# A gated hybrid decoder layer on one core: where the high and low halves of Q, K and the value differences are made, and how far ahead the weight forms stand

## The reference

```
h = rms_norm(x);  u_pool, z_pool, q, k, v, z_attn, gate_logits = split(h @ w_in)
y_pool = pool_mixer(u_pool) * silu(z_pool)            # means over 2, 4, 8, 16 tokens
attn   = stick_breaking(q, k, v)                      # 8 heads of 64, keys before the query only
y_attn = attn * silu(z_attn);  gates = sigmoid(gate_logits + b)
x = x + (gates[0] * (y_pool @ w_pool_up) + gates[1] * (y_attn @ w_attn_up)) @ w_out
return rms_norm(x, final_g)
```

## Time and profile before

| | |
|---|---|
| median of three runs | 1765.09 us |
| the profiled execution | 1765.54 us, of it the span 1763.6 us |
| mean granted TensorE clock | 0.971 |
| stage 2 | 119 to 396 us |
| stage 3 | 396 to 1391 us |
| busy: TensorE, weight loads, VectorE, ScalarE, GpSimd | 1629.8, 1340.2, 1135.2, 787.7, 1016.7 us |

### The profile page before, as it was taken

How to read it: one execution, slowest core, us unless ns; L and a number is a source line. 1 busy time by engine, 2 the same in 40 slices (tenths; PEclk the granted TensorE clock), 3 DMA queues, 4 the chain that set the end, 5 groups by cost and what they waited for, 6 DMA issues and landing times. The chain is left out here.

```text
span 1763.6 us, 25448 instructions
## 1 busy us (share of the span) xinstructions
PE 1629.8 (92%) x8030; PEld 1340.2 (76%) x8030; DVE 1135.2 (64%) x1506; ACT 787.7 (45%) x1544; POOL 1016.7 (58%) x777
## 2 busy tenths in 40 slices
PE   7999999995988988989978899898899989999998
PEld 6878888883877867768767778777778778888886
DVE  6736428903876877868878777778877774242323
ACT  4412223322565655556655566655566542111111
POOL 3521116625677888787876887888877441414140
PEclk8999999998998999999989999999999999999999
DMA  6743226765232223232474323332222575434331
GB/s 233 230 153 132 73 96 238 268 212 185 71 92 72 85 79 101 78 92 81 136 265 165 99 85 97 93 87 82 87 70 69 178 226 178 134 128 137 135 97 72
DMA packets 142679, 228.85 MB, mean 130 GB/s; under 512 B 46929, under 2 KB 63825, under 8 KB 142562
## 3 DMA queue, kind: packets, MB, share of 16 engines
q1 hardware_dynamic: 142562, 227.42, 39.8%
HBM read 149.76 MB, written 77.60 MB: 129 GB/s over the span
## 5 line engine op out<-in xcount | busy, mean ns | idle before, releaser
L1547 DVE TENSOR_TENSOR_SCAN left<-keep,left 128x512 f32<-128x512 f32 x192 | 305.0, 1589 | 72.8 <-issue 51.7
L1362 PE MATMUL psum<-hT,ring 128*128 128x512 f32 x644 | 268.8, 417 | 31.7 <-POOL ring L1612 27.3
L1366 PE MATMUL psum<-hT,ring 128*128 128x512 f32 x644 | 267.2, 415 | 0.0
L1364 PE MATMUL psum<-hT,ring 128*128 128x512 f32 x644 | 266.6, 414 | 0.0
L1612 POOL TENSOR_TENSOR ring<-raw,ring 128x512 fp32r<-128x512 f32 x161 | 253.0, 1572 | 23.4 <-POOL raw L1612 0.4
L1466 ACT ACTIVATE keep<-psum 128x512 f32<-128x512 f32 (+3 forms) x320 | 170.4, 532 | 193.8 <-PE psum L1389 192.4
L1409 PEld LDWEIGHTS psum<-wt,vm 128*128 128x128 f32 x1088 | 170.6, 194 | 100.9 <-DVE wt L1553 79.7
L1409 PE MATMUL psum<-wt,vm 128*128 128x256 f32 x1088 | 192.4, 292 | 55.2 <-DVE wt L1553 52.8
L1473 ACT ACTIVATE wt<-psum 128x512 fp32r<-128x512 f32 (+3 forms) x320 | 169.7, 530 | 95.6 <-PE psum L1398 92.8
L1553 DVE TENSOR_TENSOR wt<-psum,wt 128x512 fp32r<-128x512 f32 (+3 forms) x320 | 190.1, 594 | 32.4 <-ACT wt L1473 29.7
L1544 DVE TENSOR_TENSOR_SCAN left<-keep,floor 128x512 f32<-128x512 f32 (+3 forms) x128 | 137.8, 1077 | 66.4 <-ACT keep L1466 65.4
(11 more groups left out here) (155 smaller groups left out, 3280.5 us busy)
## 6 DMA issues: line engine op xcount, KB each, us to landing
raw<-in_w_strips SPq DMA_DIRECT2D x92, 256.0 KB, 3.1
hT<-form_scratch SPq DMA_DIRECT2D x44, 512.0 KB, 6.3
form_scratch<-t_parts SPq DMA_DIRECT2D x32, 512.0 KB, 3.8
gate_scratch<-staging SPq DMA_DIRECT2D x64, 256.0 KB, 3.2
gate<-gate_scratch SPq DMA_DIRECT2D x64, 256.0 KB, 3.9
xt<-in_x SPq DMA_DIRECT2D x16, 512.0 KB, 5.1
xT<-in_x_T SPq DMA_DIRECT2D x16, 512.0 KB, 4.0
qk_scratch<-staging SPq DMA_DIRECT2D x32, 256.0 KB, 3.0
```

Source lines behind the costliest of these rows:

```text
L1362: pe.matmul(o, hi, m_hi, start=k == 0, stop=False)
L1364: pe.matmul(o, hi, m_lo, start=False, stop=False)
L1366: last = pe.matmul(o, lo, m_hi, start=False, stop=k == HK - 1)
L1547: dve.tensor_tensor_scan(left[:, n % 4, span][:, ::-1], k, k, carry, ALU.mult, ALU.bypass).then_inc(scanned, 1)
```

## The change

Halves move from stage 3 to stage 2. After ScalarE's copy of a Q or K unit VectorE subtracts it from PSUM (`low_strip`), and both halves are stored; TensorE takes the bank again after VectorE's operation. The values come back from HBM in 16 tiles of 128 tokens at the units of `V_SLOTS`: VectorE makes the difference, ScalarE the high half, GpSimd the low half (`value_lo`), and both are stored to a new scratch. VectorE's rounds of forms now stand between the units, 6 operations after one and 4 after the next. Stage 3 loads ready halves into 5 buffers for K, 4 for V and 3 for Q, and ScalarE and GpSimd no longer touch them; a load waits for the scores or weighings of the unit that had the buffer. Four K, four V and two Q units are loaded in stage 2 already (before: two, two and one). The raw weight blocks of a group have two sets of buffers, the split of form w is placed right after the part that frees its ring slot, `weigh` runs four steps after `score` instead of three with three buffers for its operand (and three instead of four for the scan's result), and the parts are put together in four buffers, so that some waits on GpSimd's join fall one part later. Stage 4's first buffers lie elsewhere.

The diff, cut to its core:

```diff
+    KN, VN, QN = 5, 4, 3
...
+        self.km = sb("km", [P, self.KN, CH], F32R)
+        self.vm = sb("vm", [P, self.VN, CH // P, 2 * HD], F32R)
+        self.qm = sb("qm", [P, self.QN, 2, 2 * P], F32R)
...
+            sp.dma_start(self.km[part * HD:(part + 1) * HD, u % self.KN, :].bitcast(F32),
+                         self.qk_d[part, PAIRS + pair, e * HD:(e + 1) * HD, c * CH:(c + 1) * CH]
+                         ).then_inc(self.k_in[u % self.KN], DMA)
...
+            sp.dma_start(self.vm[:, u % self.VN, :, part * HD:(part + 1) * HD].bitcast(F32),
+                         self.vp_d[part, c * CH:(c + 1) * CH, cols].rearrange("(a q) d -> q a d", q=P)
+                         ).then_inc(self.v_in[u % self.VN], DMA)
...
+            self.load_k(sp, 0, u, 0, NC - 1 - u)
+            self.load_q(sp, 0, u, 0, TT // 2 - 1 - u)
+            self.load_v(sp, 0, u, 0, NC - 1 - u)
+        for u in range(2, NC):
+            self.load_k(sp, 0, u, 0, NC - 1 - u)
+            self.load_v(sp, 0, u, 0, NC - 1 - u)
...
             def put_qk(n, c):
-                put(qk_d[n - G, :, c * CH:(c + 1) * CH], use_of["qk", n, c])
+                slot = use_of["qk", n, c] % 2
+                sp.wait_ge(staged_lo, qk_order[n, c] + 1)
+                for part, src in enumerate((store[:, slot, :], store_lo[:, slot, :].bitcast(F32))):
+                    sp.dma_start(qk_d[part, n - G, :, c * CH:(c + 1) * CH], src).then_inc(stored[slot], DMA)
+                if (n, c) in V_SLOTS:
+                    t = V_SLOTS.index((n, c))
+                    if t >= 1:
+                        put_v(t - 1)
+                    if t + 1 < TT:
+                        load_v(t + 1)
+
+            def load_v(t):
+                if t >= 2:
+                    sp.wait_ge(v_lo, t - 1)
+                for i in range(2):
+                    sp.dma_start(v_raw[:, t % 2, i, :], v_d[t * P + 1 - i:(t + 1) * P + 1 - i, :]).then_inc(v_in[t % 2], DMA)
+
+            def put_v(t):
+                sp.wait_ge(v_lo, t + 1)
+                for part in range(2):
+                    sp.dma_start(vp_d[part, t * P:(t + 1) * P, :], v_parts[:, t % 2, part, :].bitcast(F32)
+                                 ).then_inc(v_stored[t % 2], DMA)
...
+            put_v(TT - 1)
             for i in range(2):
-                sp.wait_ge(stored[i], use_of["qk", G + PAIRS + 1, 0] // 2 * DMA)
+                sp.wait_ge(v_stored[i], TT * DMA)
+                sp.wait_ge(stored[i], stored_upto[use_of["qk", G + PAIRS + 1, 0] + i])
             head_loads.load_first(sp)
...
-                act.activation(store[:, use % 2, :], psum[:, c % 2, :], ACT.Copy).then_inc(staged, 1)
+                act.activation(store[:, use % 2, :].bitcast(F32R), psum[:, c % 2, :], ACT.Copy).then_inc(staged, 1)
+                if (n, c) in V_SLOTS:
+                    t = V_SLOTS.index((n, c))
+                    act.wait_ge(v_diff, t + 1)
+                    if t >= 2:
+                        act.wait_ge(v_stored[t % 2], t // 2 * 2 * DMA)
+                    act.activation(v_parts[:, t % 2, 0, :], v_raw[:, t % 2, 0, :], ACT.Copy).then_inc(v_hi, 1)
...
+            def value_lo(t):
+                pool.wait_ge(v_hi, t + 1)
+                pool.tensor_tensor(v_parts[:, t % 2, 1, :], v_raw[:, t % 2, 0, :], v_parts[:, t % 2, 0, :].bitcast(F32),
+                                   ALU.subtract).then_inc(v_lo, 1)
...
                 for c in range(NC):
+                    if (n, c) in V_SLOTS:
+                        value_lo(V_SLOTS.index((n, c)))
                     for v in t_slot(n, c):
...
+            def low_strip(n, c):
+                use = use_of["qk", n, c]
+                dve.wait_ge(staged, use + 1)
+                dve.tensor_tensor(store_lo[:, use % 2, :], psum[:, c % 2, :], store[:, use % 2, :],
+                                  ALU.subtract).then_inc(staged_lo, 1)
+                if (n, c) in V_SLOTS:
+                    t = V_SLOTS.index((n, c))
+                    dve.wait_ge(v_in[t % 2], (t // 2 + 1) * 2 * DMA)
+                    dve.tensor_tensor(v_raw[:, t % 2, 0, :], v_raw[:, t % 2, 1, :], v_raw[:, t % 2, 0, :],
+                                      ALU.subtract).then_inc(v_diff, 1)
...
+            for c in range(1, NC):
+                low_strip(G, c)
+            for c in range(NC):
+                low_strip(G + 1, c)
+                if c == 0:
+                    dve.wait_ge(mixed, 4 * G)
+                    dve.wait_ge(pool_lo, G)
+            for n in range(G + 2, G + 6):
+                for c in range(NC):
+                    low_strip(n, c)
+                    m = (n - G - 2) * 2 + c // 2
+                    (first_forms if c % 2 == 0 else last_forms)(m)
+            for n, c in units[-9:-1]:
+                low_strip(n, c)
...
-                        pe.wait_ge(staged, use_of["qk", before_n, before_c] + 1)
+                        pe.wait_ge(staged_lo, qk_order[before_n, before_c] + 1)
...
+    T_LAG, AV_LAG = 2, 4
+    LOAD, SOON = 4, 12
     ROWS = 2 * TT
+    LN, WN = 3, 3
     ROW_OF = {}
...
     def freed(w):
         return free_part[w] if w < RING else PLAIN + w - RING
 
     def split_step(w):
-        return max(fin[freed(w)], fin[PLAIN + w - AHEAD_OF[w % FORMS]]) + 1
+        return fin[freed(w)] + 1
...
+    V_LOAD = [max(K_LAST[u - VN] + AV_LAG + 1 if u >= VN else 0, K_FIRST[u] - SOON) for u in range(PAIRS * NK)]
+    Q_LOAD = [max(Q_LAST[u - QN] + 1 if u >= QN else 0, Q_FIRST[u] - SOON) for u in range(PAIRS * NQ)]
 
...
+    sum_a, sum_b, sum_c, sum_d = (sb(f"sum_{n}", [P, CH]) for n in "abcd")
...
-    block_in = {b: sem(f"s3_w_in{b}") for b in (A11, A12, S3, A22)}
+    block_in = [sem(f"s3_w_in{i}") for i in range(2)]
...
             def load_k(u):
-                e, c, _before = kv_units[u % NK]
-                hold(k_lo, u - 1)
-                head_loads.load_k(sp, (0, u // NK), u, e, c)
+                if u >= KN:
+                    hold(scored, K_LAST[u - KN] + 1)
+                head_loads.load_k(sp, u // NK, u, *kv_units[u % NK])
 
             def load_v(u):
-                e, c, _before = kv_units[u % NK]
-                hold(v_lo, u - 1)
-                head_loads.load_v(sp, (0, u // NK), u, e, c)
+                if u >= VN:
+                    hold(weighed, K_LAST[u - VN] + 1)
+                head_loads.load_v(sp, u // NK, u, *kv_units[u % NK])
 
             def load_q(u):
-                e, r = q_units[u % NQ]
-                hold(q_lo, u - 1)
-                head_loads.load_q(sp, (0, u // NQ), u, e, r)
-
-            def load_block(g, b, after):
-
-                if g == 1:
+                if u >= QN:
+                    hold(scored, Q_LAST[u - QN] + 1)
+                head_loads.load_q(sp, u // NQ, u, *q_units[u % NQ])
+
+            def load_blocks(g):
+
+                if g <= 2:
                     hold(part_done, 2)
                 else:
-                    hold(w_lo_done, split(g - 1, after) + 1)
-                a, kh = {A11: (0, 0), A12: (0, 1), S3: (1, 0), A22: (1, 1)}[b]
-                sp.dma_start(blocks[b][:, :, :], w_strips[strip_of(g, a)][:, kh * HK:(kh + 1) * HK, :]
-                             ).then_inc(block_in[b], DMA)
+                    hold(w_lo_done, split(g - 2, A22) + 1)
+                for b, a, kh in ((A11, 0, 0), (S3, 1, 0), (A22, 1, 1), (A12, 0, 1)):
+                    sp.dma_start(raws[g % 2][b][:, :, :], w_strips[strip_of(g, a)][:, kh * HK:(kh + 1) * HK, :]
+                                 ).then_inc(block_in[g % 2], DMA)
...
+                pe.wait_ge(k_in[t % KN], (t // KN + 1) * 2 * DMA)
+                pe.wait_ge(q_in[u % QN], (u // QN + 1) * 2 * DMA)
                 cols = slice(i % 2 * P, i % 2 * P + P)
-                keys = slice(c * CH, c * CH + w)
-                pe.matmul(bank_s(n)[:, 0:w], qm_hi[:, u % QN, cols], km[:, keys], start=True, stop=False)
...
+                pe.matmul(bank_s(n)[:, 0:w], qm[:, u % QN, 0, cols], keys, start=True, stop=False)
+                pe.matmul(bank_s(n)[:, 0:w], qm[:, u % QN, 1, cols], keys, start=False, stop=True).then_inc(scored, 1)
 
...
+                pe.wait_ge(v_in[t % VN], (t // VN + 1) * 2 * DMA)
                 if first:
                     wait(pe, row_done, row - 1)
                 for j in range(w // P):
...
-                wait(act, weighed, n - 1)
-                act.activation(wt[:, n % 2, 0:w // P, 0, :], bank_t(n)[:, 0:w].rearrange("p (j q) -> p j q", q=P),
+                wait(act, weighed, n - WN + 1)
+                act.activation(wt[:, n % WN, 0:w // P, 0, :], bank_t(n)[:, 0:w].rearrange("p (j q) -> p j q", q=P),
...
+                        wait_used(dve, 4 * g - 3)
                 elif j == S3:
-                    dve.wait_ge(joined, 2 * (g - 1) + 1)
+                    to = sum_d
                     dve.wait_ge(summed, 5 * (g - 1) + 2)
+                    if g > 1:
+                        wait_used(dve, 4 * g - 1)
                 elif j == S4:
```

(2 more changed lines are left out.)

379 lines of the change are left out of this document (149 added, 230 removed).

## The result

The changed kernel takes 1718.61 us in the median (1716.97 to 1720.86 in four runs), the kernel before beside it 1765.13 (1761.80 to 1766.08): a ratio of 0.9741, 95% interval 0.9723 to 0.9758, so 46.5 us faster. Forecast were 1697.5 us, with a range from 1655 to 1750. The profiled execution has a span of 1717.4 us at a mean granted clock of 0.977.

The account below looks back on a forecast made before the run. It took TensorE to bound stage 2, and stage 3 to lose time to TensorE waits behind a late GpSimd and to lowered clock. 1765.5 - 80 (steady part) - 15 (opening) + 27 (stage 2) = 1697.5 us, range 1655 to 1750.

Parts of the forecast that it names:

- the low half and the ring: Stage 3 sign: TensorE's waits on the weights' low half and the ring of weight forms fall under 25 us together.
- Steady part, -80: Stage 3 after its opening: fewer TensorE waits and less lost clock gain 80 us, bounds 46 and 107.
- They come from a late GpSimd: Stage 3: TensorE's 15 long waits, 47.2 us, come from late GpSimd through ScalarE's queue or the ring; 42 us go.
- Opening, -15: Start of stage 3: ready K, Q and V halves gain 15 us, bounds 8 and 20, though ScalarE's chain stays.
- 6 for two further steps of TensorE: Start of stage 3: TensorE gets two steps further before it needs ScalarE, gaining 6 us.
- Second stage, +27: Stage 2: TensorE goes at VectorE's pace, 14.6 us a pair of units instead of 10.9; loss 27 us, bounds 11 and 41.
- 1 us where SyncE issues 20 first loads instead of 10: End of stage 2: the doubled first loads of K, Q and V cost 1 us.
- less about 4 us that TensorE is ahead: Stage 2: TensorE's lead takes about 4 us off the loss of 30 us over eight pairs.
- Full DMA queues: Stage 2, strips 6 to 9: full queues alone would set about 12 us a pair of units.
- become the bound of the third stage: Rival for stage 3: VectorE becomes the bound, steady gain only its lower bound; 1736.5 us, chance 0.17.
- rival 2: Stage 2: TensorE's gaps bring the clock down, all 16 units at half clock cost 87 us; 1757.5 us, chance 0.09.
- Loads of K, Q and V: Rival for stage 3: late loads at each change of half, 14 loads costing 106 us; 1803.5 us, chance 0.08.

Follow-up runs that it names:

- run 6: Kernel before, with most of GpSimd's work on K, Q and V in stage 3 left out: 1737.8 us, 0.9846.
- run 7: Changed kernel with the weight forms split at the later steps of the kernel before: 1772.1 us, 1.0040 to the kernel before.
- run 4: Changed kernel weighing three steps behind the score, two operand buffers and four for the scan's result: 1746.7 us, 0.9910 to the kernel before.
- run 5: Kernel before, with only the weighing moved to four steps behind, three buffers each for operand and scan result: 1780.3 us, 1.0093.
- run 8: Kernel before, with only each weight form split right after the part that frees its ring slot: 1793.2 us, 1.0144.
- run 10: Changed kernel with one set of raw weight blocks instead of two: 1776.9 us, 1.0057 to the kernel before.
- run 9: Kernel before, with early split of weight forms and most of GpSimd's stage 3 work on K, Q and V left out: 1751.2 us, 0.9915.
- run 1: Changed kernel, stage 2: ScalarE copies the next unit before the forms' high halves; GpSimd's low halves and SyncE's stores reordered too: 1712.2 us, 0.9713 to the kernel before.
- run 3: Changed kernel with most of stage 2's value differences and low halves cut to 8 columns: 1709.7 us, 0.9691 to the kernel before.

## Why the prediction was right, and where it was not

The time fell into the range and into the forecast's own range (1670 to 1725), 21 us above the number. Most marks it named are there: no wait of ScalarE on a value difference, 15 us of waits on the low half and the ring outside the opening (asked: under 25), the third stage at 902 us (900), the clock at 0.99 in its steady part. Two are missed: GpSimd is at 604 us in the steady part and 614 in the whole stage, where below 600 was asked, and the second stage took 324 us where 304 was. Two errors stand in it, one of reason in the third stage, which luck covered, and one of size in the second.

- **Steady part, -80: measured about -86** (the scores' sigmoids stand 38.7 us later than before at item 10, 47.0 earlier at item 319). The number is near and its reason is mostly wrong, so the agreement is luck. The step that failed is "They come from a late GpSimd", taken as a GpSimd with too much to do, whose relief was to end 42 us of long waits and 23 of lost clock. Three fifths of that relief gave 27 us (run 6), and all of it with the later weighing, the second set of blocks and the fourth sum gave 35 (run 7). The later weighing, costed as part of the cover, is worth 28 in the changed kernel (run 4) and -15 alone (run 5). The early split, for which the prediction had half a sentence, is worth 54 (run 7) and -27 alone (run 8), and the second set of blocks, which it did not price, 58 (run 10). What replaces that step is the order in GpSimd's queue: block sums and forms behind joins that wait, and products and joins behind block sums (run 7), and blocks that have landed when their turn comes (run 10). How much of this held up the kernel before is open: its joins waited 37.4 us too, but no run there had the second set. Open also is the fourth sum with its later joins, which the prediction put at nothing. It was not tried apart, and where it is missing the early split ends in waits for just those joins (72 us in run 8, 56 in run 9). The parts do not add; the early split and the later weighing lose where the rest is missing.
- **Opening, -15: measured -8.5.** The chain stayed, as written. Its first weight block is copied 23.1 us after the stage opens (466.32 less 443.2), before 29.4 (425.44 less 396): 6.3 us earlier where the term had 8, and of the 6 for two further steps of TensorE 2 came.
- **Second stage, +27: measured +50.** TensorE does go at VectorE's pace, and the number for the pairs of strips 6 to 9 is right: forecast 14.6 us and 30, measured 14.7 and 28.1. Its parts are not, so the number is partly luck: VectorE is busy for some 11.7 us of a pair (82.5 of 104), of it about 9 for the round that was put at 12.0, and its waits for ScalarE's two copies are 2.4 to 3.3 us, not 1.2, because the copy stands behind high halves of the forms VectorE has just made. The mis-sized terms are "1 us where SyncE issues 20 first loads instead of 10", which was about 13 us with the clock, and "less about 4 us that TensorE is ahead": the copies were 5.6 us later in strip 5, behind a value tile that VectorE waited for. A further 4 us came from a weight strip that was 4.59 us late at 389 us, behind the same forms in ScalarE's queue. The sum had no term for the clock of this stage, which cost about 14 of the 50 us by the estimate above.
- **Full DMA queues** were put at about 12 us a pair. At 307 GB/s with a share of 0.89 (the changed kernel, 282 to 386 us) the same 4.5 million bytes would need about 13.0, an estimate, so the queues were nearer than the prediction had them.
- **Rivals.** VectorE did not become the bound of the third stage: 737 busy of 867 us. The clock in stage 2 fell behind single waits and not for whole units, so rival 2 came in part. Loads of K, Q and V cost TensorE 1.2 us.
- The rule of the Trainium skill ("SBUF — State Buffer", section "SBUF: two separate sides"), that a VectorE operation with two SBUF inputs and a GpSimd operation that reads SBUF exclude each other, agrees with run 1: with no idle time left, VectorE's operations on SBUF averaged up to 1.87 us in a group, while its low half, which reads PSUM once, stayed at 0.68.

## What to carry to other kernels

When a queue's engine is late, ask what stands in front of the late instruction before asking how much the engine has to do: here moving weight forms ahead of waiting joins, with a second set of buffers behind it, was worth more (50 us of the steady part) than everything else in that stage together, GpSimd's relief in full included (35). Parts of such a change may each lose alone, so a test of one part in the old kernel does not price it in the new one. A burst of DMA issues is a stretch in which SyncE stores nothing: count it against the number of buffers that wait for a store.

## What the runs showed of the hardware

- One DMA issue by SyncE took about 0.6 us in a row of 20 (12.1 us in all), and while it lasted no store went out.
- The DMA queues carried 328 GB/s at a busy share of 0.95 over 104 us (run 3); in the opening, 8 loads of 512 KB issued at 443.5 us held back a 256 KB load issued at 447.3 until 457.6.
- The granted clock behind a wait did not follow from the wait's length alone. Four stretches of the changed kernel, behind waits of 2.20, 3.20, 2.14 and 9.95 us (columns as above):

```profile
314.60:320.00 5.40, 5.35 (x24) 4.43 (x24) 4.22 (x8) 1.72 (x3) 1.70 (x3) 1.00 1.02 391
329.10:334.00 4.90, 4.88 (x15) 3.87 (x16) 4.90 (x6) 0.52 (x1) 1.39 (x1) 0.65 0.42 106
344.00:349.00 5.00, 4.97 (x15) 3.99 (x16) 3.58 (x6) 1.72 (x3) 1.30 (x3) 0.66 1.01 403
424.10:429.00 4.90, 4.89 (x12) 3.85 (x13) 0.69 (x1) 1.54 (x2) 1.35 (x1) 0.50 1.01 395
```

On this scale full speed is 2.4 GHz and 0.50 is 1.2. The stretch behind the 2.20 us lost nothing, and the one behind 2.14 us, 30 us later, lost two thirds of what the one behind the longest wait lost.
